# A slot for loaded weights exchanged for a slot of split half chunks

## The reference

```
mod = silu(c) @ w_ada + b_ada                 # w_ada (2048, 6144) per layer
shift, scale, gate = split(mod, 3)
h = rmsnorm(x, norm_pre) * (1 + scale) + shift
z = h @ w_in                                  # w_in (2048, 14336) per layer
gb, gcin, u, g_c, q, k, v, g_r = split(z)
y_conv = gb * causal_conv(gcin * u) * silu(g_c)
y_ret  = groupnorm(retention(rope(q), rope(k), v)) * silu(g_r)
o = concat(y_conv, y_ret) @ w_out             # w_out (4096, 2048) per layer
x = x + gate * rmsnorm(o, norm_post)
```

## Time and profile before

| what | value |
|---|---|
| median of three runs | 1758.98 us (1757.27 to 1761.2) |
| the profiled execution's own time | 1756.66 us |
| its span in the trace | 1754.9 us |
| PE busy | 1706.0 us, 97% |
| DVE busy | 1123.2 us, 64% |
| ACT busy | 720.3 us, 41% |
| moved by DMA | 414.61 MB, mean 236 GB/s |
| mean granted clock of PE | 0.993 |

### The profile page before, as it was taken

One profiled execution on the slowest core, in us unless ns is written; L12 is line 12 of the kernel. 1 busy time (PEld: TensorE's weight loads), 2 busy tenths in 40 slices (PEclk: granted clock), 3 DMA queues, 4 the chain that ended last, 5 costly groups with the idle time before them and its releaser, 6 DMA issues. The chain is left out here.

```text
span 1754.9 us, 18929 instructions
## 1 busy us (share of the span) xinstructions
PE 1706.0 (97%) x7763; PEld 1394.7 (79%) x7763; DVE 1123.2 (64%) x1291; ACT 720.3 (41%) x814; POOL 37.8 (2%) x78
## 2 busy tenths in 40 slices
PE   5899999999999999999989999999999999999998
PEld 2676888888888888878878888888888888887886
DVE  2568866778777865667776545555555555466776
ACT  2333444543444444433344444444434444433332
POOL 3000000000000000000000000000000000000000
PEclk9999999999999999999999999999999999999999
DMA  9898655777788667677874555555555555558775
GB/s 342 319 345 309 229 174 191 269 272 277 264 296 285 248 235 246 222 281 287 287 264 144 174 192 191 170 191 188 186 182 187 186 188 175 187 204 309 284 281 189
DMA packets 223174, 414.61 MB, mean 236 GB/s; under 512 B 7392, under 2 KB 40560, under 8 KB 222320
## 3 DMA queue, kind: packets, MB, share of 16 engines
q1 hardware_dynamic: 222240, 413.17, 68.0%
q10 hardware_dynamic: 848, 0.24, 0.1%
HBM read 411.28 MB, written 2.10 MB: 236 GB/s over the span
## 5 line engine op out<-in xcount | busy, mean ns | idle before, releaser
L697 DVE TENSOR_TENSOR w_lo<-stage,w_hi 128x1024 fp32r<-128x1024 f32 x574 | 693.9, 1223 | 525.3 <-ACT w_hi L531 523.7
L531 ACT CAST w_hi<-stage 128x1024 fp32r<-128x1024 f32 x574 | 596.5, 1052 | 957.0 <-PE Z L1114 591.1
L1112 PE MATMUL Z<-w_hi,H 128*128 128x512 f32 x1784 | 704.2, 395 | 13.2 <-DVE w_lo L697 10.1
L1114 PE MATMUL Z<-w_hi,H 128*128 128x512 f32 x1784 | 696.5, 390 | 0.0
L1113 PE MATMUL Z<-w_lo,H 128*128 128x512 f32 x1784 | 695.7, 390 | 0.0
L1112 PEld LDWEIGHTS Z<-w_hi,H 128*128 128x128 f32 x1784 | 336.0, 188 | 90.3 <-issue 8.9
L1114 PEld LDWEIGHTS Z<-w_hi,H 128*128 128x128 f32 x1784 | 335.5, 188 | 71.3
L1113 PEld LDWEIGHTS Z<-w_lo,H 128*128 128x128 f32 x1784 | 336.1, 188 | 68.0
L718 DVE SCALAR_TENSOR_TENSOR acc<-stage,c_silu,acc 128x512 f32<-128x512 f32 x240 | 180.2, 751 | 6.8
L1112 PE MATMUL Z<-w_hi,YR 128*128 128x512 f32 x256 | 101.9, 398 | 5.0 <-DVE w_lo L697 5.0
L1112 PE MATMUL Z<-w_hi,YC 128*128 128x512 f32 x256 | 102.2, 399 | 0.0
(11 more groups left out here) (140 smaller groups left out, 685.1 us busy)
## 6 DMA issues: line engine op xcount, KB each, us to landing
stage<-in_w_in SPq DMA_DIRECT2D x192, 1024.0 KB, 5.1
stage<-in_w_ada SPq DMA_DIRECT2D x96, 1024.0 KB, 7.5
stage<-in_w_out SPq DMA_DIRECT2D x64, 1024.0 KB, 7.4
stage<-in_w_in SPq DMA_DIRECT2D x64, 512.0 KB, 4.7
xt<-in_x SPq DMA_DIRECT2D x2, 1024.0 KB, 6.7
dec<-decay SPq DMA_DIRECT2D x8, 256.0 KB, 5.7
rows<-in_b_ada SPq DMA_DIRECT2D x2, 1024.0 KB, 4.7
rows<-in_norm_post SPq DMA_DIRECT2D x2, 1024.0 KB, 7.5
```

The lines of the kernel that those rows point to most:

```text
L531: N.copy(w_bufs(n, h)[0], stage[:, slot_of(n), 2 * h:2 * h + 2, :]).then_inc(s_hi, 1)
L697: V.tensor_tensor(lo, stage[:, slot_of(n), 2 * h:2 * h + 2, :], hi.bitcast(F32), ALU.subtract)\
L1112: T.matmul(z[:, i, :], hh, wh, start=ch.first and a == 0, stop=False)
L1114: ins = T.matmul(z[:, i, :], hl, wh, start=False, stop=stop)
```

## The change

Two constants change. The stage has three slots of 1 MB and the ring five half chunks. Load i now waits for load i - 3 to be used up, and a cast waits for the half chunk five places back. The same memory is used in all, and no instruction is added, removed or moved on any engine; only what the waits wait for is another.

```diff
-SLOTS = 4
-RING = 4
+SLOTS = 3
+RING = 5
```

## The result

| | before | after |
|---|---|---|
| median, us (4 runs each) | 1758.12 (1753.96 to 1761.2) | 1970.4 (1969.87 to 1973.33) |
| ratio to before, 95% interval | | 1.1217 (1.1193 to 1.1241) |
| span of the profiled execution, us | 1754.9 | 1968.9 |
| PE busy, us | 1706.0 | 1778.0 |
| mean granted clock of PE | 0.993 | 0.953 |

The forecast was 1932 us, from 1870 to 1990. The time lies 38 us above it. 29 us more than forecast arose in the front, 11 in the turns of layer 0 and 4 in the output stages, and the 6 us set aside for side work and the clock are in these. Each term of the kernel is compared with its forecast further down.

A forecast was written before the change was run, and what follows sets the result against it. The kernel was taken as bound by PE's matmuls, with the lost slot making loads set the pace in places: turns 76, out blocks 84, front 9, side work and clock 6 make 175 on 1756.7, so 1932 us, range 1870 to 1990.

The forecast's parts named there:

- the front: Chunks 0 to 20: loses mostly while it fills, a pair of chunks costing 14.1 us; 9 us, bounds 0 and 25.
- the turns: Chunks 39 to 100, where ada loads share the slots: PE starts chunk 100 76 us late, 62 of them by chunk 82.
- the output stages: Out blocks with gate loads: 57.4 us a block against 44.42; 42 us per layer, 84 us for both.
- side work: Casts, copies and rotations in the turns, mostly hidden while transfers are awaited; 6 us together with PE's clock, bounds 0 and 40.
- the clock: PE at 1.2 GHz after a wait loses 1.7 us, hidden while loads set the pace; within 6 us shared with side work.
- The prices of the chain: Turns and out blocks: between successive ada or gate loads used up, 11.6, 14.4, 17.0, 20.1 us for one to four chunks.
- The steady stretches: Chunks 100 to 111 and 146 to 255, with only w loads: keep their time, some 6 us of slack left.
- the rival of the falling clock: PE's clock low so often after waits that PE is late too; 1990 to 2170 us, 5%.
- signs of being wrong: Two chunks with an ada or gate load between under 12 us, the steady stretch waiting, or granted clock below 0.95.
- The ring: Fifth half chunk against PE's 15.1 us of low-half waits: taken as 0, bounds -15 and 0, beside 2.7 us earlier starts.
- The milder rival: The turns' loads overlap better and only out blocks bind fully; 1850 us, range 1800 to 1890, 12%.
- the one that was not slower: The ring's fifth half replaces the slot and PE's 15.1 us of waits go; 1742 us, 3%.

The follow-up runs named there:

- the shorter use: Against the changed kernel (three slots, ring of five), DVE makes one of the four products of each ada and gate load; 1831.4 us, ratio 1.0432.

## Why the prediction was right, and where it was off

**The prices of the chain: right.** Reckoned from rows of the output stage before the change, they met the means of the three shorter distances, 59 of the 61 links, to within 0.2 us; the single link that was furthest off took 15.9 us where I had 14.4. The cause is shown by the order (182 us back when A and w change places) and by the shorter use (links of one and two chunks took 9.2 and 12.1 us instead of 11.6 and 14.5). The Trainium skill, "DMA: Bandwidth & Descriptors", section Anatomy of one DMA, states its 2.0 us plus bytes over 436 GB/s for transfers that GpSimd issues, and these are issued by SP. By it the sum would have been 1888 us, 82 below the time; the trace's 5.1 us was the better price. The advice to issue early, which I named with it, stands in that page's Rules for kernel authors.

**The turns: 87.4 measured, 76 forecast.** 3.7 us come from the 23 links between chunks 39 and 82, each 0.16 us longer in the mean than reckoned. The distances of four took 22.8 us, not 20.1, which makes 5.4 us for two: PE had no wait from 657.2 to 680 us nor from 724 to 748, so that its own pace bound there, where I had written that a distance of four wins something back. The last 1.7 us arose at chunk 100 itself, which took 7.1 us instead of 5.4: the clock was low from 783.5 to 786.9 us.

**The output stages: 88.3 measured, 84 forecast.** Right; 1 us of it arose at the boundary between the layers.

**The steady stretches: right,** to 0.1 us over 110 chunks of layer 1.

**The front: 38.4 measured, 9 forecast, and outside its bounds of 0 and 25.** Walking load by load I had 4 us at chunk 2, 6 at chunk 7 and 9 at chunk 18; the traces have 7.4, 14.2 and 36.8. The first 4.0 us were there at chunk 0, where the walk had put nothing: with three slots the last of the eight A loads ahead of chunk 0 goes out at 30.0 us instead of 22.6, and PE waits for its landing, which it didn't do before.

```profile
35.20 1.26 PE L1149 MATMUL A<-stage,c_cols 128*32 128x512 f32 x8 [3.52 <-DMA stage<-in_w_ada]
```

The step that failed is the sum "landing to PE's start 2.4, one chunk 5.5, the A's matmuls 1.0, the next transfer 5.1: 14.1 us" for a pair of chunks (the four terms make 14.0). Three of its terms were too small. Here is one such pair, chunk 13 to chunk 15, and the window of its first chunk:

```profile
167.90 0.50 PE L1112 MATMUL Z<-w_hi,H 128*128 128x512 f32 x1 [2.20 <-DVE part L864]
...
175.18 1.07 PE L1149 MATMUL A<-stage,c_cols 128*32 128x512 f32 x8
...
176.31 0.37 SPq L478 DMA_DIRECT2D stage<-in_w_ada  x1
176.72 0.51 SPq L506 DMA_DIRECT2D stage<-in_w_in  x1
...
184.37 1.99 ACT L531 CAST w_hi<-stage 128x1024 fp32r<-128x1024 f32 x2 [10.88 <-DMA stage<-in_w_in]
...
187.86 0.79 PE L1112 MATMUL Z<-w_hi,H 128*128 128x512 f32 x1 [4.95 <-DVE part L864]
```

```profile
167.90:175.18 7.28, 7.28 (x24) 5.56 (x24) 6.09 (x10) 4.21 (x8) 1.61 (x2) 0.77 0.65 208
```

From 167.90 to 187.86 it is 20.0 us. PE's chunk took 7.3 us until 175.18 where I had 5.5: the clock, granted at 0.77 in this stretch. The freed slot took the next A load, and the w load went out behind it, its cast at 184.37, 8.1 us after 176.31 where I had 5.1: the same price of a pair that I had used in the turns and overlooked here. And the start of PE, 3.5 us after the cast instead of 2.4, waited for DVE's addition (L864), which came behind the low half. The experiments show two of the three: the addition, together with ACT's copy in the first group (chunk 28 9.7 us earlier in the trace with the order turned round), and the clock (9.0 us of the whole time). That the w load goes second I read from the rows, and no run took it away. With both out of the way chunk 28 still starts 19 us late (253.78 against 234.58), 5 of which were there at chunk 0 in that trace; the rest is not divided further.

**The clock** I had called hidden, at 1.7 us a dip, because the loads set the pace. In the turns and output stages that holds but for the 1.7 us at chunk 100: links of up to three chunks kept their length with the clock at 0.91 to 0.95. It doesn't hold in the front, where PE itself frees every other A slot: there a slower PE makes the next load later, and that makes PE wait. The rival of the falling clock was thus right in the front alone, at some 9 us. What the Trainium skill, "TensorE: Matmul & The Clock Gate", section HAM oscillation, tells of a kernel that waits for DMA between groups of matmuls, each of which starts at half clock, is seen here in part: the clock fell at most of PE's longer waits, though not at all of them, and was low for 187 us of the trace in all. But the time stayed 20 us under that rival's range of 1990 to 2170. Nor was it one dip before the change: that trace has six low stretches, 27 us in all. One of my signs of being wrong was met in part: of the four runs two were granted less than 0.95 in the mean (0.949 and 0.947), the others 0.95 and 0.953.

**That the total fell into the range** was in part luck. The front overran its own bound, and the range held because its upper end had room for side work of up to 40 us that didn't arise. Of the other signs, two A loads two chunks apart never took under 12 us and the steady stretch didn't wait, but PE awaited low halves in 45 places for 129 us, not in some 60 for over 150: some of PE's waiting stood in other rows, 13.5 us for DVE's additions (L864, 3.1 before) and 10.4 us for ACT (L636).

**The ring:** its fifth half is worth 0 to 10 us beside three slots in the whole time, where I had taken 0 beside the earlier starts of the chains. **PE's busy time** I expected nearly unchanged; it rose by 72 us, which the clock can account for: it was at half for 161 us more than before, up to 80 us of PE's work. **The milder rival and the one that was not slower** are both excluded by the table of links.

## What to carry to other kernels

Before a slot is taken from a prefetch store, look for transfers of a second kind in its order, and ask for each what frees its slot: two transfers that wait for one another in a row set a chain. Here it ran while the DMAs' busy share fell from 0.80 to 0.64, so rate to spare didn't shorten it. A load that is used up after its neighbour belongs behind it in the queue; here that was worth 182 us with three slots and 8.5 us with four. Where the engine that waits also frees the slots, its clock belongs in the sum.

## What the runs showed of the hardware

The granted clock fell to half during or just after single waits of PE of 1.8 to 6.2 us, between long runs of matmuls (mean 0.94 in the block from 965 to 1021 us, the third output block, which had 1.00 before). It didn't do so at each: a wait of 3.2 us that ended at 1047.9 us left it at 1.00. Extra matmuls, 76 in the whole front, put where PE had waited, kept it at 1.00 from 66 to 215 us. The w_in loads of 1 MB took 5.1 us from issue to landing in the median, with four slots and with three.
